# A fused transformer mixer: first chunk transposed before its scales are known, and three orders changed

## The reference, cut to what matters

```python
x = x + pos_embed_2d(n)                              # row table | column table
sh_x, sc_x, gt_x = modulation(c, w_mod, b_mod)       # silu(cond) @ w_mod + b_mod
sh_c, sc_c, gt_c = modulation(c_ctx, w_mod, b_mod)
hx = rmsnorm(x, g_pre) * (1 + sc_x) + sh_x
hc = rmsnorm(ctx, g_pre) * (1 + sc_c) + sh_c
ux = hx @ w_in                                       # 1024 -> 2304, seven parts
vc_lru = hc @ w_in[:, :W_LRU]
y_lru_x, y_lru_c = lru_branch(vx_lru, vc_lru, ...)   # conv of 4, gates, two scans
y_pool_x = pool_mixer(vx_pool, pool_w, pool_scale)
y_conf_x = conformer_conv(vx_conf, ggx_conf, ...)    # GLU, conv of 31, LayerNorm, swish, product
o_x = merge_out(...)                                 # times silu of gates, @ w_out
return x + gt_x * rmsnorm(o_x, g_post)
```

## Time and profile before

| what | value |
|---|---|
| time, median of 3 runs (lowest, highest) | 780.63 us (776.61, 785.11) |
| the profiled execution | 782.04 us |
| its span in the trace | 780.0 us |
| PE busy | 726.6 us (93%), 3548 instructions |
| DVE busy | 520.5 us (67%) |
| ACT busy | 463.5 us (59%) |
| POOL busy | 266.0 us (34%) |
| mean granted TensorE clock | 0.967 of full |
| DMA | 130.10 MB, mean 167 GB/s |

### The profile page before, as it was taken

One profiled execution on the slowest core, in us unless ns is written; L12 is line 12 of the kernel. 1 busy time (PEld: TensorE's weight loads), 2 busy tenths in 40 slices (PEclk: granted clock), 3 DMA queues, 4 the chain that ended last, 5 costly groups with the idle time before them and its releaser, 6 DMA issues.

```text
span 780.0 us, 10037 instructions
## 1 busy us (share of the span) xinstructions
PE 726.6 (93%) x3548; PEld 568.5 (73%) x3548; DVE 520.5 (67%) x767; ACT 463.5 (59%) x756; POOL 266.0 (34%) x302
## 2 busy tenths in 40 slices
PE   3886989999998999999999989899999999999997
PEld 1574867767776778767877767667787888888885
DVE  4277653655999698897997755686646575756422
ACT  4266653699887987897887992324554142534311
POOL 0022234233442355433544256313211144434421
PEclk9597999999999999999999999989999999999999
DMA  9999012443354545345464045244469768867531
GB/s 360 364 291 282 15 41 83 109 110 112 109 162 117 160 156 169 118 121 141 141 194 139 34 155 152 74 145 137 134 211 313 229 198 275 302 202 249 178 127 63
DMA packets 89217, 130.10 MB, mean 167 GB/s; under 512 B 22768, under 2 KB 54128, under 8 KB 87632
## 3 DMA queue, kind: packets, MB, share of 16 engines
q1 hardware_dynamic: 84800, 115.44, 45.5%
q0 software_dynamic: 4368, 14.03, 6.7%
HBM read 91.17 MB, written 38.27 MB: 166 GB/s over the span
## 4 chain that ended last, share of the span: by engine, by line
PE 49%; ACT 18%; DVE 16%; DMA 7%; issue 6%; POOL 2%; SPq 1%; DVEq 0%; ACTq 0%; POOLq 0%
PE bank L1507 15%; PE bank L1508 15%; PE bank L1509 15%; DMA wm<-in_w_mod 3%; ACT Ib L918 3%; ACT Ab L930 2%; ACT rb L932 2%; ACT Qb L931 2%; DVE xc L1110 2%; DVE gacc L1110 2%; ACT L930 2%; DVE Qb L1110 2%; DVE xg L1170 1%; DVE Qb L1279 1%; DVE yrow L1279 1%
## 5 line engine op out<-in xcount | busy, mean ns | idle before, releaser
L1507 PE MATMUL bank<-xTh,wh 128*128 128x512 f32 (+1 forms) x592 | 238.8, 403 | 10.8 <-DVE xTl L1178 3.8
L1509 PE MATMUL bank<-xTh,wl 128*128 128x512 f32 (+1 forms) x592 | 231.4, 391 | 0.0
L1508 PE MATMUL bank<-xTl,wh 128*128 128x512 f32 x576 | 227.1, 394 | 0.0
L1507 PEld LDWEIGHTS bank<-xTh,wh 128*128 128x128 f32 x592 | 112.8, 190 | 46.3 <-issue 15.6
L1509 PEld LDWEIGHTS bank<-xTh,wl 128*128 128x128 f32 x592 | 112.7, 190 | 23.8
L1508 PEld LDWEIGHTS bank<-xTl,wh 128*128 128x128 f32 x576 | 109.9, 191 | 21.8 <-issue 1.2
L1507 PE MATMUL bank<-xTh 128*128 128x512 f32 (+1 forms) x272 | 104.2, 383 | 1.6 <-issue 1.1
L1509 PE MATMUL bank<-xTh,xTl 128*128 128x512 f32 x256 | 99.6, 389 | 0.0
L1508 PE MATMUL bank<-xTl,xTh 128*128 128x512 f32 x256 | 99.6, 389 | 0.0
L904 ACT ACTIVATE ustage<-bank 128x512 f32<-128x512 f32 x56 | 32.5, 591 | 74.2 <-PE bank L1509 69.8
L1110 DVE SCALAR_TENSOR_TENSOR Qb<-Qb,rb 128x512 f32<-128x512 f32 (+1 forms) x40 | 41.0, 1037 | 43.6 <-ACT rb L932 43.6
(11 more groups left out here) (189 smaller groups left out, 1416.1 us busy)
## 6 DMA issues: line engine op xcount, KB each, us to landing
scratch_u<-ustage SPq DMA_DIRECT2D x72, 256.0 KB, 3.5
wraw<-in_w_in SPq DMA_DIRECT2D x18, 512.0 KB, 5.1
wm<-in_w_mod SPq DMA_DIRECT2D x8, 1024.0 KB, 14.2
xg<-in_x SPq DMA_DIRECT2D x16, 512.0 KB, 9.0
yb<-scratch_y SPq DMA_DIRECT2D x32, 256.0 KB, 3.4
gb<-scratch_u SPq DMA_DIRECT2D x32, 256.0 KB, 4.8
xres<-in_x SPq DMA_DIRECT2D x16, 512.0 KB, 4.7
out<-tout SPq DMA_DIRECT2D x15, 512.0 KB, 3.0
```

Source lines behind the costliest of these rows:

```text
L1507: mm(out, wh_, xh_, start=first, stop=False)
L1508: mm(out, wh_, xl_, start=False, stop=False)
L1509: return mm(out, wl_, xh_, start=False, stop=last)
```

## The change

There are four edits.

1. *Front.* SP loads the context rows, the column table, the first chunk's rows and its row table ahead of all modulation blocks. The context and the first chunk are normalised and transposed as they are; TensorE does the chunk's transposes between modulation products, in three PSUM banks that those leave free (`tp0`). ScalarE copies the transposed slices back over the rows (`keep`, to `kept(gi, k)`), and `modulate` later reads them there. The high part of the first weight moves behind this on ScalarE and so do the low parts on VectorE. The squares of the first two groups write their discarded result to `fbuf`. The second chunk's adds and squares, which were spread over the first chunk's slices, come partly behind them, and the third chunk's column adds behind the second chunk's normalising.
2. *Piece.* `conv(here + 4)` at step s = 1 moves ahead of that step's GLU and squared term.
3. *Sum of squares.* `ln_lo(n - 1)` moves behind `ln_square_sum(n)`.
4. *Output wait.* The wait for the last evacuations moves from before the first output tile to before the third.

```diff
+        tp0 = bank[1:4]
...
             a = (g - 1) * CH + i * P
             return xg[:, k0:k1, a:a + P]
 
+        def kept(g, k):
+            return cbuf[:, :, k, :] if g == 0 else xg[:, k, 0:CH]
+
         def phases(ap, n):
 
             return ap.rearrange("p (j n) -> p j n", n=n)
...
                     sp.wait_ge(s_of, n + 1 + h)
                     sp.dma_start(out[n * P:(n + 1) * P, hs], tout[:, n % 2, hs]).then_inc(s_out[n % 2], 16)
 
+            load_rows(0)
+            sp.dma_start(posc[:], pos_col).then_inc(s_posc, 16)
+            load_rows(1)
+            load_pos(1)
+            load_w(0)
             for m in range(8):
                 sp.dma_start(wm[:, m], w_mod[m]).then_inc(s_wm[m], 16)
-                if m == 0:
-                    load_w(0)
-                if m == 1:
-                    load_rows(0)
                 if m == 5:
                     load_w(1)
             load_w(2)
-            sp.dma_start(posc[:], pos_col).then_inc(s_posc, 16)
-            load_rows(1)
-            load_pos(1)
             load_w(3)
             load_rows(2)
             load_pos(2)
...
                         act.wait_ge(s_ssum, gi)
                     if T:
                         act.wait_ge(done, T)
-                    a.activation(slices(junk[h][:]), rows(gi, i, 4 * h, 4 * h + 4), ACT.Square,
+                    a.activation(slices(junk[h][:] if gi > 1 else fbuf[:, h, :]), rows(gi, i, 4 * h, 4 * h + 4), ACT.Square,
                                  accum_out=sq2[:, 2 * i + h:2 * i + h + 1]).then_inc(done, 1)
 
             def root(gi):
                 act.wait_ge(s_ssum, gi + 1)
                 n = GROUPS[gi][1]
                 a.activation(rst[:, 0:n], ssq[:, 0:n], ACT.Sqrt, bias=epsc, scale=1.0 / D).then_inc(s_sd, 1)
+
+            def keep(gi):
+                n = GROUPS[gi][1] * P
+                for k in range(KD):
+                    idx = 8 * gi + k
+                    act.wait_ge(s_tp, idx + 1)
+                    src, dst = tp0[idx % 3][:, 0:n], kept(gi, k)
+                    a.activation(dst, slices(src) if gi == 0 else src, ACT.Copy).then_inc(s_kept, 1)
 
             def modulate(gi, ks=range(KD)):
                 n = GROUPS[gi][1] * P
                 so = mo + (16 if gi == 0 else 0)
                 for k in ks:
                     idx = 8 * gi + k
-                    act.wait_ge(s_tp, idx + 1)
+                    if gi < 2:
+                        act.wait_ge(s_kept, idx + 1)
+                    else:
+                        act.wait_ge(s_tp, idx + 1)
                     if idx >= 4:
                         act.wait_ge(s_hh, idx - 3)
                         act.wait_ge(s_hl, idx - 3)
-                    a.activation(fbuf[:, idx % 4, 0:n], tp[idx % 4][:, 0:n], ACT.Identity,
+                    else:
+                        act.wait_ge(s_ssum, 2)
+                    src, dst = kept(gi, k) if gi < 2 else tp[idx % 4][:, 0:n], fbuf[:, idx % 4, 0:n]
+                    a.activation(slices(dst) if gi == 0 else dst, src, ACT.Identity,
                                  scale=col(so + k), bias=col(so + 8 + k)).then_inc(s_f, 1)
 
             def evac(U):
...
                 a.activation(x_, x_, ACT.Sigmoid).then_inc(s_cgs, 1)
 
             first, second = range(0, KD // 2), range(KD // 2, KD)
-            w_hi(0)
             for h in range(2):
                 squares(0, h, range(CTX // P))
             root(0)
+            squares(1, 1)
+            keep(0)
+            squares(1, 0)
+            root(1)
+            w_hi(0)
+            keep(1)
             w_hi(1)
             w_hi(2)
             act.wait_ge(s_sc, 1)
             modulate(0)
-            squares(1, 1)
-            evac(0)
-            w_hi(3)
-            squares(1, 0)
-            evac(1)
-            root(1)
-            evac(2)
             for k in range(KD):
                 modulate(1, [k])
-                squares(2, 1 - k // TPC, [k % TPC])
+                if k == 1:
+                    w_hi(3)
+                if k == 3:
+                    evac(0)
+                if k == 6:
+                    evac(1)
+            squares(2, 1)
+            evac(2)
+            squares(2, 0, range(0, 2))
             evac(3)
+            squares(2, 0, range(2, 4))
             root(2)
             evac(N_CU)
             squares(3, 1)
...
                 v.memset(carry, 0.0).then_inc(s_sc, 1)
 
             first, second = range(0, KD // 2), range(KD // 2, KD)
-            w_lo(0)
             square_sums(0)
             normalise(0)
+            add_cols(1)
+            add_rows(1)
+            square_sums(1)
+            normalise(1)
+            w_lo(0)
             mod_rows(range(3))
             w_lo(1)
             mod_rows([3])
             scales()
+            lo_group(0, first)
             w_lo(2)
-            lo_group(0, first)
-            add_cols(1, range(0, 2))
             lo_group(0, second)
-            add_cols(1, range(2, 4))
-            add_rows(1)
-            w_lo(3)
-            square_sums(1)
-            normalise(1)
             for k in range(KD):
-                add = add_cols if k < TPC else add_rows
-                add(2, [k % TPC])
                 lo_group(1, [k])
-            add_cols(3)
+                if k == 2:
+                    w_lo(3)
+                if k >= TPC:
+                    add_cols(2, [k - TPC])
+            add_rows(2)
             square_sums(2)
             normalise(2)
+            add_cols(3)
             for gi in (2, 3):
                 for k in range(KD):
                     if k < TPC:
...
                 if s == 0:
                     if t == 0:
                         conv(2)
+                if s == 1:
+                    conv(here + 4)
                 for j in convs_in_step(q, 4):
                     conv_glu(j)
                 one_minus_a2(q)
...
                     conv_z_lo(j)
                 if GATES_AFTER[q] + 1 in WEIGHTS_BEHIND_GATES:
                     weights_lo(GATES_AFTER[q] + 1)
-                if s == 1:
-                    conv(here + 4)
                 scans(q)
                 weights_lo(min(STEP_END[q], GATES_AFTER[-1]))
                 if q in GATE_STEP:
...
                     ln_sum(n)
                 if kind == "sq":
                     ln_square_sum(n)
+                    if n:
+                        ln_lo(n - 1)
                 if kind == "mu":
                     ln_centre(n)
                 if kind == "var":
                     if n + 1 < NCH:
                         ln_sum(n + 1)
                     ln_norm(n)
-                if kind == "swish":
+                if kind == "swish" and n == NCH - 1:
                     ln_lo(n)
                 if kind == "wo":
                     out_weights_lo(n)
...
                     ins = mm(bank[0][:, 2 * mt:2 * mt + 2], mrow[:, mt * P:(mt + 1) * P], par_col("sel", 0, 2), start=True, stop=True)
                 ins.then_inc(s_modT, 1)
 
-            pe.wait_ge(s_par, 16)
-            for m in range(4):
-                mod_product(2 * m)
-                mod_product(2 * m + 1)
-                if m:
-                    mod_turn(m - 1)
-            mod_turn(3)
-
             def transposes(gi, ks=range(KD)):
                 pe.wait_ge(s_xh, gi + 1)
                 if gi == 0:
                     pe.wait_ge(s_id, 2)
                 for k in ks:
                     idx = 8 * gi + k
-                    if idx >= 4:
+                    to = tp0[idx % 3] if gi < 2 else tp[idx % 4]
+                    if gi < 2 and idx >= 3:
+                        pe.wait_ge(s_kept, idx - 2)
+                    elif idx >= 20:
                         pe.wait_ge(s_f, idx - 3)
                     for i in range(GROUPS[gi][1]):
-                        ins = nc.tensor.transpose(tp[idx % 4][:, i * P:(i + 1) * P],
-                                                  rows(gi, i, k, k + 1)[:, 0, :], ident[:])
+                        ins = nc.tensor.transpose(to[:, i * P:(i + 1) * P], rows(gi, i, k, k + 1)[:, 0, :], ident[:])
                     ins.then_inc(s_tp, 1)
 
             def project(U, h, l, xh, xl, n, low_from=None, between=None):
...
                 ins.then_inc(s_pg, 1)
 
             transposes(0)
+            pe.wait_ge(s_par, 16)
+            for m in range(5):
+                mod_product(m)
+            transposes(1, range(0, 3))
+            mod_product(5)
+            mod_turn(0)
+            transposes(1, range(3, 6))
+            mod_product(6)
+            mod_turn(1)
+            transposes(1, range(6, 8))
+            mod_product(7)
+            mod_turn(2)
+            mod_turn(3)
+            pe.wait_ge(s_kept, 2 * KD)
             pe.wait_ge(s_sc, 1)
             for U in range(N_CU):
                 pe.wait_ge(s_wlo, U + 1)
                 h, l = early_w(U)
                 project(U, h, l, xTh[:, :, c3:c3 + CTX], hcl[:], CTX, 0 if U == 0 else None)
-            transposes(1)
```

(4 more changed lines are left out.)

## The result

The changed kernel takes 783.84 us (median of 20 runs, 779.01 to 788.9); the kernel before took 780.25 us over 20 runs (776.61 to 785.11). The ratio is 1.0036 with a 95% interval of 1.002 to 1.0052: 2.8 us slower, between 1.6 and 4.1. The forecast was 2.0 us faster. The profiled execution of the changed kernel has a span of 782.6 us, that of before 780.0. Its lines are numbered 27 higher on TensorE (L1534 is L1507 of before), 24 on most of VectorE (L1134 is L1110) and 17 on ScalarE's evacuations.

A forecast was written before the change was run, and what follows sets the result against it. No single engine was taken to bound the kernel; the chain passes from loads through chunk preparation and scan loops to TensorE. +6.2 - 5.4 - 1.7 - 1.1 = -2.0 gave median 778.6 us, 8-in-10 range 770 to 788.

The forecast's parts named there:

- Loads: At the start: row loads and tables ahead of the last modulation block take 10.9 us, moving its completion from 30.3 to 41.2.
- (a): Rival, chance 0.20: TensorE stays at half clock during modulation, scales at 56.1, front costs 11.8, piece worth 4; total 785.6.
- (d): Rival, chance 0.04: the new order does not take hold, slice copies wait and weights are blocked; scales beyond 58, above 788.
- After the scales: From scales to the normalised second chunk: 28.5 us in place of 38.4, ready at 79.0, 3.6 later than before.
- the 0.6: First chunk's first unit waits for the third context evacuation behind squares; its own evacuation holds ScalarE perhaps 0.6 us more.
- the front: Loads to first scaled slice of the second chunk: 3.6 + 2.0 + 0.6 = +6.2 us, staying lost afterwards.
- The piece: Four scan blocks: moving a 2.9 us convolution piece ahead of the squared term gives -5.4 us, bounds -1.6 and -9.
- such waits: Sign of being wrong: new TensorE waits for evacuations between 250 and 340 us, giving back the piece's gain.
- The first block: First scan block: VectorE's 5.55 us wait hides the piece; 1.6 us gained for the loop, 1.79 for TensorE.
- The sum of squares: Tail: TensorE's 3.82 us wait ending at 508.71 gives -1.7 us, bounds 0 and -4; a 2 us `lsl` wait remains.
- the output wait: Before the output product: two tiles' products cover the evacuation, -1.1 us of 1.12, or 0 if something else is late.
- The sum: Whole kernel: front, piece, sum of squares and output wait total -2.0 us; 782.0 becomes 780.0, median 778.6.

The follow-up runs named there:

- e4: Front alone on the kernel before, with ScalarE's third and fourth context evacuations each ahead of four squares of the third chunk: ratio 1.0007, +0.5 us (-1.3 to +2.3).
- e5: e4 plus two VectorE orders: column adds ahead of the sum of squares, a weight's low part behind the scales; against the kernel before 0.9973, -2.1 us.
- e9: Kernel before with the piece moved up in the second scan block only: ratio 1.0043, +3.4 us (+1.6 to +5.1).
- e2: Kernel before with only the piece moved up, in all four scan blocks: ratio 1.0031, +2.4 us (+0.4 to +4.4).
- e11: Changed kernel with the front of e5 and GpSimd's load behind its multiplications, piece in all blocks; against the kernel before 0.9961, -3.0 us, median 777.87.
- e12: e8 with GpSimd's load of the next block's first piece behind its two multiplications; against the kernel before 0.9907, -7.3 us, median 773.44.
- e3: Kernel before with the tail only (sum of squares and output wait edits): ratio 0.9963, -2.9 us (-5.0 to -0.9).
- e1: Kernel before with the whole front only; piece, sum of squares and output wait as before: ratio 1.0019, +1.5 us (-0.4 to +3.4).
- e8: Kernel before with the front of e5, the tail, and the piece in the first block only: ratio 0.9914, -6.7 us (-9.1 to -4.3), median 775.85.
- e7: Kernel before with the piece moved up in the first scan block only: ratio 0.9987, -1.0 us (-2.7 to +0.8).
- e10: Kernel before with only GpSimd's load of the next block's first piece behind its two multiplications: ratio 0.9991, -0.7 us (-2.3 to +0.9).
- e6: Kernel before with the piece moved up in all blocks and GpSimd's load behind its multiplications: ratio 1.0001, +0.1 us (-1.3 to +1.6).

## Why the prediction was wrong

**Loads: right.** Block 4's product was forecast at 31.5 and began at 30.92; the last product began at 42.3, with its block there. Rivals (a) and (d) did not happen: the scales came at 48.3, forecast 50.3. The last turn ended at 46.98, 2.0 us earlier than the 49.0 of my sum. One reading was loose: the 7.80 us of the earlier trace rows is SP's time to issue four row loads, not their transfer; at the 290 GB/s of the earlier trace rows their 2.10 MB take 7.2.

**After the scales: too long, then too short.** The way to the normalised second chunk was forecast at 28.5 and was 26.7. From there to the first scaled slice I had 1.4 + 2.0 and 0.6 for the evacuation, 4.0; it was 5.5. The mechanism of the 0.6 (the first unit waits for the third context evacuation behind the squares) was the right one and mis-sized. I had counted only the evacuation on ScalarE, and neither TensorE's 4.13 us of idleness nor the clock of 0.66 behind it; e4 takes both away and its first scaled slice comes 1.7 us sooner behind the scales. In sum the front was forecast at +6.2; the traces show +3.2 at 139 us, and alone it was timed at +1.5 (-0.4 to +3.4), of which e5 turns the sign.

**The piece: wrong, and this is the step that failed.** The forecast was -5.4 with bounds of -1.6 and -9. Measured: +2.4 (+0.4 to +4.4). For the second block the prediction said that "the loop gains nothing and the roots come later, but TensorE's 2.80 goes; ScalarE waited 3.63 us for TensorE at 303.71, so that lead can be used". That wait lies 54 us behind the place and is no lead: in the kernels whose roots are late it did not shrink, at 3.62 us in the changed kernel, 3.63 in e9 and 5.21 in e2. The roots came 3.1 us later (e9), the evacuations behind them were late too, and TensorE had to wait for a weight and for evacuations from 250 to 302: 5.2 us for 2.80. The text named such waits as what would prove it wrong, and its lower bound let them take back a gain; it had no case in which they cost more than they gave, and both bounds were gains. That the piece costs is shown in time by e2, e9 and the pair e11 and e12. The way from late roots to the whole of that cost is argued, since the traces of e9 and e11 do not show it at the end of the scan stage. The first block, worth 1.6 in the forecast, was timed at -1.0 (-2.7 to +0.8); the third has a wait of 2.94 in place of 1.05 at 418, which no run looked at alone.

**The sum of squares and the output wait: right.** -2.8 forecast, -2.9 (-5.0 to -0.9) measured, and the wait for `lsl` is 2.53 where 2 was forecast. e3 did not time the two apart.

**The sum.** +6.2 - 5.4 - 1.7 - 1.1 = -2.0 was forecast; the parts alone give +1.5 + 2.4 - 2.9 = +1.0, each within about 2 us, and the whole +2.8 (+1.6 to +4.1). Two errors of opposite sign hid each other in part: the front was 3 to 5 us too dear and the piece 8 too cheap. Rival (a), at 785.6, came near the measured 783.84 by luck, for its slow modulation did not happen. The chance of 0.06 for slower by over 1% was not the trouble; that no rival priced a piece that costs was.

## What to carry to other kernels

Work moved up on an engine that has no idle time in that stretch can delay the next engine's work by its own length (2.9 us of piece, roots 2.7 to 3.1 us later), however small the waits are that it removes; look at what stands directly behind it in the same queue, and price the way to where the delay comes back. A later wait of the engine that is made late is slack only if it shrinks when the work comes late; here it stayed at 3.6 us or grew. Where the moved work falls into idle time (here the first block) the same edit can be made for that block alone; it did not cost there, though its gain alone was not separated from none. When a front is re-ordered, follow each thing that the critical engine needs next to the small operation that frees or makes it, and look what stands ahead of that in its queue: three such places made the difference between +1.5 and -2.1 us.

## What was not expected of the hardware

The same wait of TensorE is sometimes followed by a lower clock and sometimes not. In the kernel with the tail alone and in that with the front alone the wait for the convolution in the second block is 2.83 and 2.81 us long. The stretch around each (us, PE busy, PEclk, DMA share, GB/s), tail alone first:

```profile
250.00:260.00 10.00, 10.00 (x52) 0.84 0.89 271
```

```profile
250.00:260.00 10.00, 7.20 (x48) 1.00 0.90 262
```

The kernel before has 0.83 there. At half clock for a third of ten microseconds this is some 1.7 us, and it is where e1 wins back its 1.7 between 250 and 334 us (82.06 us for that way, 83.72 before). Of the nine traces with this wait, five have the lower clock behind it (before, e3, e5, e8, e12) and four do not (e1, e4, e7, e10). The five with the piece ahead in this block (the changed kernel, e2, e6, e9, e11) have a mean clock of 1.00 from 240 to 300 us. Single traces of this kernel can so differ by as much as a part of the change is worth; the timed ratios, not the traces, carry the sums above.
